# Mask and bias added with the row maximum in two attentions, and neighbourhood heads taken in pairs

## What is computed

```python
# first block: 16 heads of 64, 272 keys, 2 blocks of 128 queries
s = einsum("bthd,bshd->bhts", q, k) * 64**-0.5 + (c_q[..., :, None] - c_k[..., None, :])   # c = cumsum(log f)
p = softmax(where(kpos <= qpos, s, -inf));   o = einsum("bhts,bshd->bthd", p, v)

# second block, twice: 8 heads of 64, 4 rows of 64 columns, window of 16 columns
s = einsum("bjqhd,bijkhd->bhjqik", q_row, k_band) * 64**-0.5
s = where(col_mask, s + bias, -inf);   w = softmax(s);   out = einsum("bhjqik,bijkhd->bjqhd", w, v_band)
```

## Time and profile before

| | us |
|---|---|
| median of 3 runs | 2070.25 |
| profiled execution, its own time | 2069.78 |
| its span (first to last instruction) | 2068.1 |
| forgetting attention, PE from scores of pair 1 to the first output product | 382.25 to 426.67 |
| neighbourhood attention of layer 0, first score to first output product | 553.58 to 575.64 |
| neighbourhood attention of layer 1 | 887.77 to 909.83 |

### The profile page before, as it was taken

One profiled execution on the slowest core, in us unless ns is written; L12 is line 12 of the kernel. 1 busy time (PEld: TensorE's weight loads), 2 busy tenths in 40 slices (PEclk: granted clock), 3 DMA queues, 4 the chain that ended last, 5 costly groups with the idle time before them and its releaser, 6 DMA issues.

```text
span 2068.1 us, 29412 instructions
## 1 busy us (share of the span) xinstructions
PE 2040.6 (99%) x11021; PEld 1704.5 (82%) x11021; DVE 1578.4 (76%) x1399; ACT 1267.9 (61%) x1272; POOL 162.6 (8%) x134
## 2 busy tenths in 40 slices
PE   9999999999999999999999999999999999999998
PEld 8977897778889998987778888888888888888876
DVE  6867444577766557768989888888988888898887
ACT  6766533453545334465677777777777777777774
POOL 0032020001114000021300000000000000000100
PEclk9999999999999999999999999999999999999999
DMA  6533594237546555826999999999999999999995
GB/s 242 186 114 102 187 361 168 90 107 264 178 142 228 186 183 172 280 75 231 350 412 383 368 383 367 370 381 369 381 367 384 367 372 379 370 380 370 386 382 211
DMA packets 88066, 580.43 MB, mean 281 GB/s; under 512 B 10144, under 2 KB 13472, under 8 KB 22064
## 3 DMA queue, kind: packets, MB, share of 16 engines
q1 hardware_dynamic: 79472, 548.26, 70.5%
q0 software_dynamic: 7904, 29.95, 4.1%
q10 hardware_dynamic: 608, 1.07, 0.1%
HBM read 559.96 MB, written 15.73 MB: 278 GB/s over the span
## 4 chain that ended last, share of the span: by engine, by line
PE 92%; DVE 4%; issue 1%; DMA 1%; ACT 1%; POOL 0%; DVEq 0%; ACTq 0%; SPq 0%
PE bank L643 84%; PE bank L1416 1%; DMA ring<-in_w_moe 1%; DVE wrest L2634 1%; PE bank L858 1%; PE bank L1219 1%; DVE wrest L2043 0%; PE bank L947 0%; PE bank L861 0%; PE bank L1387 0%; PE bank L977 0%; PE bank L1033 0%; PE bank L1226 0%; DMA cst<-in_consts 0%; PE bank L957 0%
## 5 line engine op out<-in xcount | busy, mean ns | idle before, releaser
L2634 DVE TENSOR_TENSOR wrest<-ring,whi 128x2048 fp32r<-128x2048 f32 x378 | 853.2, 2304 | 75.2 <-ACT whi L1942 74.5
L1942 ACT ACTIVATE whi<-ring 128x2048 fp32r<-128x2048 f32 x374 | 698.2, 1918 | 76.2 <-DMA ring<-in_w_moe 72.3
L643 PE MATMUL bank<-whi,xgT 128*128 128x512 f32 x1008 | 405.0, 402 | 1.9 <-DVE wrest L2634 1.8
L643 PE MATMUL bank<-wrest,xgT 128*128 128x512 f32 x1008 | 396.0, 393 | 0.0
L643 PE MATMUL bank<-whi,xgR 128*128 128x512 f32 x1008 | 393.5, 390 | 0.0
L643 PEld LDWEIGHTS bank<-whi,xgR 128*128 128x128 f32 x1008 | 189.5, 188 | 46.9
L643 PEld LDWEIGHTS bank<-whi,xgT 128*128 128x128 f32 x1008 | 189.4, 188 | 46.2 <-DVE wrest L2634 6.2
L643 PEld LDWEIGHTS bank<-wrest,xgT 128*128 128x128 f32 x1008 | 188.9, 187 | 38.8
L643 PE MATMUL bank<-whi,hidE 128*128 128x512 f32 x504 | 201.8, 400 | 1.6 <-DVE wrest L2634 1.6
L643 PE MATMUL bank<-wrest,hidE 128*128 128x512 f32 x504 | 197.8, 392 | 0.0
L643 PE MATMUL bank<-whi,hidR 128*128 128x512 f32 x504 | 196.8, 390 | 0.0
(11 more groups left out here) (485 smaller groups left out, 3705.2 us busy)
## 6 DMA issues: line engine op xcount, KB each, us to landing
ring<-in_w_moe SPq DMA_DIRECT2D x378, 1024.0 KB, 4.8
ring<-in_w_dense SPq DMA_DIRECT2D x135, 1024.0 KB, 4.9
row<-in_rows POOLq DMA_DIRECT2D x17, 512.0 KB, 5.2
xg_rows<-ncR POOLq DMA_DIRECT2D x12, 512.0 KB, 24.4
y_rows<-arena POOLq DMA_DIRECT2D x9, 512.0 KB, 5.9
arena<-xg_rows SPq DMA_DIRECT2D x9, 512.0 KB, 5.3
arena<-arena SPq DMA_DIRECT2D x32, 106.5 KB, 4.0
arena<-in_tbias POOLq DMA_DIRECT2D x2, 1536.0 KB, 8.6
```

Of the source, the lines that this page charges most:

```text
L643: ins = pe.matmul(out_, lhsT, rhs, start=start, stop=stop, **more)
L1942: S["w_hi"].on(a.activation(whi[:, n % HI_SLOTS, :], ring[:, c % RING, :], ACT.Copy))
L2634: S["w_lo"].on(v.tensor_tensor(wrest[:, s, :], ring[:, s, :], whi[:, n % HI_SLOTS, :].bitcast(F32), ALU.subtract))
```

## The change

In the forgetting attention the mask is no longer a product on PE. DVE does one instruction per head, `tensor_tensor_reduce`: bank plus `causal`, times -1, written to `prb`, and the minimum of that as the negated row maximum. ACT then takes the exponential in place in `prb` with scale -1. The bank is free when DVE is done, so PE waits for `sc_max` in place of `sc_exp`. ACT's wait for `pt_done` moves to DVE. `turn_o` comes after the weighing in its step, `copy_o` two heads later, `rest_o` two pairs later, the DVE's four rounding pieces in pairs 8, 11, 12 and 15, and `turn_meta` goes to the bank of values not in use.

In the neighbourhood attention the 1/8 is put into `q2` when it is made, `q2` has four full planes (no zeroing), and two heads' scores are two products of 64 rows each, in the two row halves. DVE does one `tensor_tensor_reduce` per head in place of two instructions. Turning, copying and weighing go by pairs; of the eight copies of 128x512 DVE does five and ACT three (`DVE_COPIES`, `ACT_COPIES`).

At the start the identity's DMA gets its own semaphore, shared with the convolution's `stack`; ACT's first squares wait only for the meta tokens.

```diff
+DVE_COPIES, ACT_COPIES = (0, 1, 3, 6, 7), (2, 4, 5)
 ...
-            pe.wait_ge(ld_meta, 32)
+            pe.wait_ge(ident_stk_in, 16)
 ...
-                    wait(pe, "sc_exp", max(u - 2, 0))
+                    if u != 5:
+                        wait(pe, "sc_max", max(u - 2, 0))
-                    pe.matmul(b[:, 0:w], ident_a[:, :], causal[:, P * (1 - j):P * (1 - j) + w], start=True, stop=False,
-                              skip_group_check=True)
 ...
-                if p >= 7 and p % 4 == 3:
-                    turn_o(p // 4 - 1)
                 if 1 <= p <= PAIRS:
                     turn_p(p - 1)
 ...
+                if p >= 7 and p % 4 == 3:
+                    turn_o(p // 4 - 1)
 ...
-                def scores2(u):
+                def scores2(p):
-                    S["s_ps"].on(pe.matmul(score_bank(u), q2[:, hh, j * P:(j + 1) * P], k2[:, hh // 2, :],
-                                           start=True, stop=True))
+                    wait(pe, "s_in", 16 * i + max(2 * p - 1, 0))
+                    for u in (2 * p, 2 * p + 1):
+                        j, hh = divmod(u, N_HEADS)
+                        r = slice(HD * (u % 2), HD * (u % 2) + HD)
+                        S["s_ps"].on(pe.matmul(score_bank(u), q2[r, hh // 2, j * P:(j + 1) * P], k2[r, hh // 2, :],
+                                               start=True, stop=True))
 ...
+                for p in range(10):
+                    if p < 8:
+                        scores2(p)
+                    if p == 1:
                         wait(pe, "p_act", 12 * (i + 1))
                         conv_spread()
+                    if 1 <= p <= 8:
+                        turn2(p - 1)
+                    if p >= 2:
+                        weigh2(p - 2)
 ...
-                a.wait_ge((ld_x, x_in, ld_meta)[t], 32 if t == 2 else 16)
+                a.wait_ge((ld_x, x_in, ld_meta)[t], 16)
 ...
-                wait(a, "pt_done", pair_count(u // 2 - 2) if u >= 4 else 0)
-                S["sc_exp"].on(a.activation(prb[:, u % 4, 0:n], fox_bank(u)[:, 0:n], ACT.Exp, bias=nmax[:, u % 4:u % 4 + 1],
-                                            accum_out=rsum[:, j, hh:hh + 1]))
+                S["sc_exp"].on(a.activation(prb[:, u % 4, 0:n], prb[:, u % 4, 0:n], ACT.Exp, scale=-1.0,
+                                            bias=nmax[:, u % 4:u % 4 + 1], accum_out=rsum[:, j, hh:hh + 1]))
 ...
-                        S["sc_max"].on(v.tensor_reduce(nmax[:, u % 4:u % 4 + 1], fox_bank(u)[:, 0:n], AX.X, ALU.max,
-                                                       negate=True))
+                        wait(v, "pt_done", pair_count(p - 2) if p >= 2 else 0)
+                        m = P * (1 - u // H_ATT)
+                        S["sc_max"].on(v.tensor_tensor_reduce(prb[:, u % 4, 0:n], fox_bank(u)[:, 0:n], causal[:, m:m + n],
+                                                              -1.0, 3e38, ALU.add, ALU.min, nmax[:, u % 4:u % 4 + 1]))
 ...
-                    fin(v.scalar_tensor_tensor(sc2[:, u % 3, :], score_bank(u), HD ** -0.5,
-                                               tb[:, hh, (2 - 2 * j) * GRID_W:(6 - 2 * j) * GRID_W],
-                                               ALU.mult, ALU.add))
                     wait(v, "s_exp", 16 * i + max(u - 3, 0))
-                    S["s_in"].on(v.tensor_reduce(nmax[:, u % 4:u % 4 + 1], sc2[:, u % 3, :], AX.X, ALU.max,
-                                                 negate=True))
+                    S["s_in"].on(v.tensor_tensor_reduce(sc2[:, u % 4, :], score_bank(u),
+                                                        tb[:, hh, (2 - 2 * j) * GRID_W:(6 - 2 * j) * GRID_W], -1.0, 3e38,
+                                                        ALU.add, ALU.min, nmax[:, u % 4:u % 4 + 1]))
+                    if u % 2 and u // 2 - 1 in DVE_COPIES:
+                        copy_t(u // 2 - 1)
```

More of the change, by code:

```diff
@@ L397, in meta_count, with copied @@
             return 5 * (q + 1)
+        def copied(i, p):
+            for name, copies, first in (("pt_done", DVE_COPIES, meta_count(3)), ("t_done", ACT_COPIES, 0)):
+                if p in copies:
+                    return name, first + len(copies) * i + copies.index(p) + 1
         half_banks = ((4, 7), (6, 5))
@@ new lines, in scores2, with turn2 @@
+                    for u in (2 * p, 2 * p + 1):
[3 more added lines that the diff above has]
+                                               start=True, stop=True))
+                def turn2(p):
+                    wait(pe, "s_exp", 16 * i + 2 * p + 2)
+                    if p >= 2:
+                        wait(pe, *copied(i, p - 2))
+                    for u in (2 * p, 2 * p + 1):
+                        for b in range(2):
+                            x = 2 * (u % 2) + b
+                            ins = pe.transpose(ps[2 + p % 2][:, x * P:(x + 1) * P], sc2[:, u % 4, b * P:(b + 1) * P],
+                                               ident)
+                    S["t_ps"].on(ins)
@@ new lines, in weigh2 @@
+                def weigh2(p):
+                    wait(pe, *copied(i, p))
+                    for u in (2 * p, 2 * p + 1):
+                        j, hh = divmod(u, N_HEADS)
+                        c = slice(hh * HD, (hh + 1) * HD)
+                        for b in range(2):
+                            x = 2 * (u % 2) + b
+                            ins = mm(ps[4 + j][:, c], p2T[:, p % 2, x * P:(x + 1) * P], v2[:, b, c],
+                                     start=b == 0, stop=b == 1, skip_group_check=True)
@@ L1827, in keys @@
                     else:
-                        for e in range(2):
-                            r = slice(e * HD, (e + 1) * HD)
-                            ins = a.activation(q2[r, 2 * (f - 12) + e, :], ps[f % 4][r, 0:SEQ], ACT.Identity,
-                                               bias=bias[r])
+                        ins = a.activation(q2[:, f - 12, :], ps[f % 4][:, 0:SEQ], ACT.Identity, bias=bias,
+                                           scale=HD ** -0.5)
                     S["p_act"].on(ins)
@@ L1865, in layer @@
                     wait(a, "s_in", 16 * i + u + 1)
-                    S["s_exp"].on(a.activation(sc2[:, u % 3, :], sc2[:, u % 3, :], ACT.Exp,
+                    S["s_exp"].on(a.activation(sc2[:, u % 4, :], sc2[:, u % 4, :], ACT.Exp, scale=-1.0,
                                                bias=nmax[:, u % 4:u % 4 + 1], accum_out=rsum[:, j, hh:hh + 1]))
-                    if u:
-                        copy_t(i, u - 1)
+                    if u % 2 == 0 and u // 2 - 1 in ACT_COPIES:
+                        copy_t(i, u // 2 - 1)
                 def copy_a(j, bank):
@@ L1913, in gate_embedding, with copy_t @@
                     S["ple_act"].on(a.activation(fe[:, j, c], fe[:, j, c], ACT.Sigmoid))
-            def copy_t(i, u):
-                wait(a, "t_ps", 16 * i + u + 1)
-                wait(a, "a_ps", 16 * i + max(u - 1, 0))
-                S["t_done"].on(a.activation(p2T[:, u % 2, :], ps[2 + u % 2][:, 0:SEQ], ACT.Copy))
+            def copy_t(i, p):
+                wait(a, "t_ps", 8 * i + p + 1)
+                wait(a, "a_ps", 8 * i + max(p - 1, 0))
+                S["t_done"].on(a.activation(p2T[:, p % 2, :], ps[2 + p % 2][:, :], ACT.Copy))
             layer(0)
@@ L2209, in rest_y @@
                 S["t_lo"].on(v.tensor_tensor(yTr[:, t, :], yT[:, t, :], yTh[:, t, :].bitcast(F32), ALU.subtract))
-            def zero_halves(q):
-                pairs = q[:, :, :].rearrange("p (f e) n -> p f e n", e=2)
-                v.memset(pairs[HD:P, :, 0, :], 0.0)
-                fin(v.memset(pairs[0:HD, :, 1, :], 0.0))
             rest_l1(GATE_FIRST + 3)
@@ L2303, in _ @@
                         wait(v, "pv_ps", meta_count(q - 1) if q else 0)
[L2304 removed]
+                        S["pt_done"].on(v.tensor_copy(pTm, ps[4 + (q + 1) % 2][:, 0:P]))
                 if p >= 6 and p % 4 == 2:
                     outputs(p // 4 - 1)
[L2307 to L2312 removed]
+                if p >= 9 and p % 4 == 1:
+                    rest_o(p // 4 - 2)
+                if p in WPA_PIECES:
+                    c, m = WPA_FIRST % RING, WPA_PIECES.index(p)
+                    x = slice(m * 512, (m + 1) * 512)
+                    if m == 0:
                         wait(v, "w_hi", WPA_FIRST + 2)
@@ L2478, in layer @@
                 rest_proj(i, 4)
-                zero_halves(q2)
+                q_bias = vec[:, v0 + VL_BK + 4:v0 + VL_BK + 8]
+                v.tensor_scalar(q_bias, q_bias, HD ** -0.5, None, ALU.mult)
                 rest_proj(i, 5)
@@ L2518, in layer, with copy_t @@
                 v.wait_ge(tb_in, 16 * (i + 1))
+                def copy_t(p):
+                    wait(v, "t_ps", 8 * i + p + 1)
+                    wait(v, "a_ps", 8 * i + max(p - 1, 0))
+                    S["pt_done"].on(v.tensor_copy(p2T[:, p % 2, :], ps[2 + p % 2][:, :]))
                 for u in range(16):
```

90 lines of the change are left out of this document (30 added, 60 removed).

## The result

The changed kernel takes 2077.54 us, the median of 20 executions (2068.05 to 2080.91); the kernel before took 2071.39 beside them (20 executions, 2069.23 to 2072.07). The ratio is 1.0026, 95% interval 1.0016 to 1.0036: slower by about a quarter of a per cent, 6 us by the medians, where I had forecast 2059.0, 11.2 us faster. The executions of the changed kernel spread over 13 us, and their mean granted clock of TensorE goes with them: 0.994 at 2068.05, 0.992 at 2070.4 to 2070.9, 0.990 at 2074.3, 0.987 to 0.988 at 2078.3 to 2080.9. The kernel before, wherever its clock was recorded in this study, has 0.997 to 0.999.

A forecast was written before the change was run, and what follows sets the result against it. The prediction took PE, 92% of the chain, to bound the kernel. Gains of 1.6 (start), 5.6 (forgetting attention) and 4.0 us (both neighbourhood attentions) made 11.2, so 2070.25 became 2059.0, range 2055 to 2066.

The forecast's parts named there:

- What bounds the kernel: Whole kernel: PE is 92% of the chain, so a change elsewhere pays only where PE waits.
- Start: Kernel start: the identity's own semaphore lets the first square start 1.6 us earlier; bounds 0 and 2.3.
- The call's length: New DVE call in both attentions: about 0.3 us for 144 elements, 0.42 for 256, 0.43 for 272.
- second instructions: DVE's write of each call's 128x1 result: 0.6 us of PE waits in forgetting attention, 0.25 per neighbourhood attention.
- (a): Rival, all three attention stretches: the new call runs at half rate, leaving a gain of 2.6, so 2067.6 us; chance 0.14.
- (b): Rival, all three attention stretches: the call has a large fixed DVE cost, 7.6 us slower, 2077.9 us; chance 0.06.
- Forgetting attention: Stretch from pair 1's scores to first output product: 44.42 to 38.8 us, a gain of 5.6; bounds 3.5 and 7.
- Neighbourhood attention: Each layer's stretch goes from 22.06 to 20.05 us, a gain of 2.0, 4.0 in both; bounds 0.5 and 3.
- Waits: 0.7 before the scores of pair 1: Neighbourhood attention: PE waits 0.7 us there, as the bank is free only when DVE has done head 0.
- Pairs in halves: Neighbourhood scores in two row halves: 0.63 us for two heads in place of 0.80 to 0.86, 1.95 per pair.
- (c): Rival: pairs bring nothing in the neighbourhood attention, latency 0.5 us longer, 4.0 us go, 2063 us; chance 0.12.
- (d): Rival, neighbourhood attention: the row halves do not run beside each other, 6.9 us go, 2066 us; chance 0.04.

The follow-up runs named there:

- before_stall: Kernel before with one added PE wait, for VectorE's maximum of head 0 ahead of head 2's neighbourhood scores: 2073.62 us against 2070.35.
- wide sums: Changed kernel with the convolution's sums taken over 64 equal columns of ones in place of one: 2058.56 us, ratio 0.9945.
- first profile: Changed kernel unaltered, profiled in one of its quickest executions: 2068.08 us.
- full8: Changed kernel with neighbourhood scores over 128 rows from eight zeroed query planes, still in pairs, and head 3's scores in idle PSUM bank 5: 2059.13 us.
- fill_wait: Changed kernel with one extra 128x512 product after pair 0's neighbourhood scores, filling PE's standstill: 2066.04 us.
- second profile of the changed kernel: Changed kernel unaltered, profiled once more: 2070.73 us, layer 0 at full clock and layer 1 at half clock for nearly the whole stretch.

## Why the prediction was wrong, point by point

**What bounds the kernel** was right: PE is 92% of the chain as in the earlier trace rows, and every us in the three stretches moved the end.

**Start**: 1.6 forecast. The transposes came 1.55 us earlier, but the half clock of the earlier trace rows went as well, which I had only used for the upper bound of 2.3, and at the first `xhi` product the gain is 2.34. The term was 0.7 us too small for this pair of profiles. Where the kernel before has no half clock at its start I estimate 1.5: `before_stall` takes 6.30 us from the transposes to `xhi` at full clock, and 11.16 + 6.30 is 17.46, against 15.93.

**The call's length** was right: 305, 422 and 438 ns for 144, 256 and 272 elements. As VectorE's time it was priced too high: the second instruction (83 ns) overlaps the next call, and calls follow each other in 0.35 us (256) and 0.37 (272), where I had 0.5 and 0.45. The terms of 0.6 us in the forgetting attention and 0.25 in each neighbourhood attention for the second instructions show up in no wait of PE. Rivals (a) and (b) are out by the rows.

**Forgetting attention**: 38.8 forecast, 38.94 measured, a gain of 5.5 for 5.6. I had 3.6 for the mask and 2.0 for fewer waits. By the view of waits PE waited 4.2 us before and 2.6 after, so 1.6 came from waits and 3.9 from the mask's products. The absolute working was off: a pair in the middle takes 2.40 us with 272 keys (410.40 to 412.80) where my paces add to 2.23, and 1.50 with 144 keys (389.77 to 391.27) for 1.34. Two decay rows take 0.41 ahead of the scores (383.01 to 383.42), not 0.24. I counted too little work and too many waits. What is missing is about the same on both sides: my 35.0 us of work and the 4.2 of waits leave 5.2 of the 44.42 before, my 31.4 and 2.6 leave 4.9 of the 38.94 after. So the gain came out right because the same error stands on both sides; which products it lies in, beyond the decay rows, no run isolates.

**Neighbourhood attention**: here is the step that failed. "Waits: 0.7 before the scores of pair 1" was right to 0.02 us as a length, and I priced it as 0.7 us. Nowhere did I ask what PE's clock does when this wait, the half-filled scores and the one-column sums come one behind the other, though the earlier trace rows had shown the half clock after an idle time. No rival had it, so the range held no such case. At full clock the term as a sum is right: 20.17 us in the changed kernel's own untouched layer, 20.18 and 20.16 in the kernel with wide sums, for 20.05. The clock costs 9.5 us over my sum in the first profile, 12.4 and 18.6 in the other two, against a forecast gain of 11.2; the median execution, 2077.54, is 19 us above the 2058.5 of a kernel with both layers at my sum.

**Pairs in halves** are worth less than I said. With halves a pair has 0.63 us of scores as forecast, but turning then takes 0.49 before the weighing and weighing 0.94 before the next scores; with 128 rows these are 0.44 and 0.84. So a pair without any wait takes 2.06, not 1.95, against 2.20 with 128 rows (0.92, 0.44, 0.84), here a pair of `full8`:

```profile
552.59 1.08 PE L1226 MATMUL bank<-arena 128*128 128x256 f32 x4
553.51 0.60 PE L1236 MATMUL bank<-cst,arena 128*128 128x128 f32 x4
553.95 1.00 PE L649 MATMUL bank<-arena 128*128 128x64 f32 x8
554.79 1.08 PE L1226 MATMUL bank<-arena 128*128 128x256 f32 x4
```

The difference of 0.14 us in sixteen pairs is the 2.2 us of experiment 8. The Trainium skill ("TensorEngine Tiling (Array Packing)", Key Properties) has the change of tiling mode drain TensorE. The trace agrees in that the turning behind the halves and the weighing ahead of them are longer than beside full rows, by 0.15 us a pair in sum; that this is the drain, no run isolates. Against this, ScalarE's copies, for which I had 0.35 and 0.30 us, cost 0.14 each, and the 0.25 for the second instructions and 0.16 of `conv_spread` (1.97 forecast, 1.81 measured at full clock) fell away. That 20.17 comes so near to 20.05 is these misses cancelling: luck in part.

**Rivals (c) and (d)** didn't occur. The pairs did their part, and the halves do overlap (0.63 us for two heads, 0.92 over 128 rows).

**The total** without the clock: 2058.56 us with wide sums, 2018.4 + 40.1 = 2058.5 from the changed kernel's own profiles, for 2059.0. The three stretches did not give this as forecast: 2.35 from the start, 5.5 and twice 1.9 make 11.6 in the traces, for 1.6, 5.6 and 4.0.

## What to carry to other kernels

A wait on TensorE has two prices: its length, and what the clock costs if it stands beside thin products; look at the granted clock over both sides of each place where a change puts a wait, a half-filled product or a one-column product near another of them, and give its loss as a rival. A one-column product of a 128x128 operand could here be made 64 columns wide for nothing, since eight of them took 1.8 us either way, and that alone turned a loss of 6 us into a gain of 11. When executions of one kernel spread while those of the kernel beside it don't, read each execution's mean clock before any theory of waits.

## What the runs showed of the hardware

- The granted clock of TensorE fell to 1.2 GHz while the engine counted as busy all the time (fill_wait, layer 1: 6.00 of 6.00 us busy up to the fall, 12.00 of 12.00 at 0.50). The Trainium skill ("TensorE: Matmul & The Clock Gate", What's actually happening) has the clock follow how busy TensorE has been. The runs agree in that filling or removing the standstill made falls rarer, and add that, at the same busy time, 64 columns in place of one in the same 1.8 us ended the falls.
- The fall is not the same from one execution to the next, nor for two equal stretches of one: 20.17 and 32.36 us for the same work in the second profile of the changed kernel.
- At half clock a pair takes 3.80 us for 2.06, so a stretch at half clock loses nearly half of its length (32.36 us with 27 at half clock, for 20.17).
- A custom VectorE call with two inputs and a reduced output takes 305, 422 and 438 ns for 144, 256 and 272 elements, as a plain two-input instruction does (421 for 256), with 83 ns for the second instruction, which overlaps the next call (0.35 us from call to call at 422 ns each).
- Two fp32 products of 64 rows and 256 columns in the two row halves take 0.63 us for 0.92 over 128 rows, but the products beside them take 0.15 us longer, so that 0.14 a pair is left.
